# A 256-token two-part model on one core: x turned by float32 products, the gates ahead of the norms, the first doubling level by a difference

## The reference, cut to what matters

```
h = rms_norm(x, norm1_g)                        # (256, 1024)
proj = h @ w_in                                 # dn_qkv, dn_z, dn_a, dn_b, ..., fox_f, gates

def gated_deltanet(qkv, z, a_logit, b_logit, conv_w, a_log, dt_bias, out_g):
    qkv = silu(causal_depthwise_conv(qkv, conv_w))
    q = l2_norm(heads(q)) * dk ** -0.5
    k = l2_norm(heads(k))
    beta = sigmoid(b_logit)
    g = -exp(a_log) * softplus(a_logit + dt_bias)
    gc = cumsum(g)                              # inside chunks of 64 tokens
    decay = exp(gc_i - gc_j) for j <= i, else 0
    lower = where(strict, (k * beta) @ k.T * decay, 0)
    sol = triangular_solve(lower + eye(64), [v * beta, k * beta * exp(gc)])
    u, w = split(sol)
    # then a scan over the four chunks with a 128x128 state per head
```

## Time and profile before

| what | before |
|---|---|
| runs, us | 1417.14, 1419.36, 1419.49 (median 1419.36) |
| the profiled execution, us | 1417.25 |
| its span, us | 1415.4 |
| mean granted clock of TensorE | 0.972 |
| busy: TensorE, VectorE, ScalarE, GpSimd | 93%, 31%, 46%, 67% |
| DMA | 218.86 MB, mean 155 GB/s |

### The profile page before, as it was taken

The page is one execution under the profiler, slowest core; times in us unless marked ns, Lnnn a source line. Parts: engine busy times, 40 slices in busy tenths (PEclk is TensorE's granted clock), DMA queues, the critical chain, the costliest instruction groups (busy, mean ns, idle before and its releaser), DMA issues.

```text
span 1415.4 us, 19665 instructions
## 1 busy us (share of the span) xinstructions
PE 1315.2 (93%) x8226; PEld 1169.4 (83%) x8226; DVE 438.4 (31%) x769; ACT 649.5 (46%) x835; POOL 953.2 (67%) x416
## 2 busy tenths in 40 slices
PE   4989999768899999999999999999999978999997
PEld 4978977647688999889789978999878846999885
DVE  3537314524423321005554232101033445010114
ACT  5562326544544654334444444444435653443533
POOL 6745236534497888885648967886966645887984
PEclk9999999978999999999999999999999999999999
DMA  7634124322355555553435575564646423654651
GB/s 260 178 101 134 61 75 130 121 63 91 122 194 164 179 187 185 194 191 101 156 102 172 198 237 164 174 191 138 221 170 210 160 90 115 183 174 140 211 206 45
DMA packets 118092, 218.86 MB, mean 155 GB/s; under 512 B 9417, under 2 KB 18932, under 8 KB 117876
## 3 DMA queue, kind: packets, MB, share of 16 engines
q1 hardware_dynamic: 114016, 210.01, 46.3%
q10 hardware_dynamic: 3988, 7.60, 1.7%
HBM read 216.53 MB, written 1.05 MB: 154 GB/s over the span
## 4 chain that ended last, share of the span: by engine, by line
PE 81%; DVE 10%; ACT 4%; issue 2%; DMA 2%; ACTq 0%; POOL 0%; SPq 0%; DVEq 0%
PE acc L1832 12%; PE acc L1834 12%; PE acc L1835 12%; PE acc L1825 10%; PE acc L1826 10%; PE acc L1827 10%; PE pm L1840 8%; PE acc L1783 2%; PE acc L1784 2%; PE acc L1785 2%; ACT pm L544 1%; DMA raw<-in_w_in 1%; PE pm L1749 1%; ACT whi L544 1%; DVE XTlo L1032 0%
## 5 line engine op out<-in xcount | busy, mean ns | idle before, releaser
L529 POOL TENSOR_TENSOR wlo<-raw,whi 128x1024 fp32r<-128x1024 f32 (+2 forms) x412 | 953.0, 2337 | 447.7 <-ACT whi L544 446.3
L544 ACT ACTIVATE whi<-raw 128x1024 fp32r<-128x1024 f32 (+2 forms) x412 | 413.2, 1020 | 391.6 <-PE acc L1827 172.6
L1832 PE MATMUL acc<-XThi,whi 128*128 128x256 f32 x1424 | 406.5, 285 | 4.8 <-issue 2.9
L1834 PE MATMUL acc<-XTlo,whi 128*128 128x256 f32 x1424 | 404.9, 284 | 0.0
L1835 PE MATMUL acc<-XThi,wlo 128*128 128x256 f32 x1424 | 404.8, 284 | 0.0
L1832 PEld LDWEIGHTS acc<-XThi,whi 128*128 128x128 f32 x1424 | 275.4, 193 | 6.2 <-issue 3.7
L1834 PEld LDWEIGHTS acc<-XTlo,whi 128*128 128x128 f32 x1424 | 275.5, 193 | 0.2
L1835 PEld LDWEIGHTS acc<-XThi,wlo 128*128 128x128 f32 x1424 | 275.4, 193 | 0.0
L1825 PE MATMUL acc<-whi,XThi 128*128 128x512 f32 (+3 forms) x336 | 134.2, 399 | 2.9 <-POOL wlo L529 2.2
L1826 PE MATMUL acc<-wlo,XThi 128*128 128x512 f32 (+3 forms) x336 | 130.0, 387 | 0.0
L1827 PE MATMUL acc<-whi,XTlo 128*128 128x512 f32 (+3 forms) x336 | 129.5, 385 | 0.0
(11 more groups left out here) (409 smaller groups left out, 1672.6 us busy)
## 6 DMA issues: line engine op xcount, KB each, us to landing
raw<-in_w_in SPq DMA_DIRECT2D x68, 512.0 KB, 3.6
raw<-in_w_ff SPq DMA_DIRECT2D x64, 512.0 KB, 3.6
raw<-in_w_in_mix SPq DMA_DIRECT2D x44, 512.0 KB, 3.5
raw<-in_w_down SPq DMA_DIRECT2D x44, 512.0 KB, 4.3
raw<-in_w_gate SPq DMA_DIRECT2D x40, 512.0 KB, 3.5
raw<-in_w_up SPq DMA_DIRECT2D x40, 512.0 KB, 3.6
raw<-in_w_branch SPq DMA_DIRECT2D x16, 512.0 KB, 3.5
raw<-in_w_out_mix SPq DMA_DIRECT2D x16, 512.0 KB, 3.5
```

What stands on the lines that cost most here:

```text
L529: nc.gpsimd.tensor_tensor(wlo[:, u % SPLIT, 0:nk, 0:width], raw[:, u % RAW, 0:nk, 0:width], whi[:, u % SPLIT, 0:nk, 0:width].bitcast(F32), ...
L544: return nc.scalar.activation(out_, in_, func, **k)
L1832: T.matmul(o, wh[:, fs], hi[:, k, :], start=opens and f % 2 == 0, stop=False, skip_group_check=True)
L1834: T.matmul(o, wh[:, fs], lo[:, k, :], start=False, stop=False, skip_group_check=True)
```

## The change

Two things are put together. **At the start**, x comes in two halves (`x_in`, `x1_in`) and the head of the constants goes to ScalarE's queue, in front of `heads` and `o_g`. VectorE no longer scales x: it makes for each half of the tokens a 128x128 diagonal matrix, the identity (which TensorE has put into `pm`, semaphore `eye`) times the inverse roots. The turn is now a float32 product of x with this matrix. ScalarE copies the gains before it splits weights, and splits units 0 and 1, makes two groups of XThi, splits unit 2, makes the other two, and goes on. The rest of the constants comes behind unit 3. **In the delta rule**, ScalarE takes the gates' exponentials ahead of the norms, and VectorE the softplus ahead of q and k, on free columns of abc's bank of PSUM. TensorE waits for `dn_qkn` rather than `dn_rn` ahead of the sums, and their difference is taken straight from PSUM. The first level is not computed by products: with X = Y = 1, Y becomes 1 - mask, a subtraction on VectorE, and X is its transpose, 8 transposes on TensorE, which ScalarE copies into `d_x`. The fills of `d_x` and `d_y` go.

The diff, with its parts on declarations and addresses left out:

```diff
         @block.sync
         def _(sp_):
-            sp_.dma_start(X[:], a["x"].rearrange("(t p) d -> p t d", p=P)).then_inc(S["x_in"], 16)
-            sp_.dma_start(ct[:, 0:HEAD_COLS], a["consts"][:, 0:HEAD_COLS]).then_inc(S["x_in"], 16)
+            sp_.dma_start(X[:, 0, :], a["x"][0:P, :]).then_inc(S["x_in"], 16)
+            sp_.dma_start(X[:, 1, :], a["x"][P:2 * P, :]).then_inc(S["x1_in"], 16)
             for u, (w, k, nk, c0, width) in enumerate(units):
-                if u == 2:
+                if u == 4:
                     sp_.dma_start(ct[:, HEAD_COLS:], a["consts"][:, HEAD_COLS:]).then_inc(S["k_in"], 16)
                 if u >= RAW:
...
                 return fn(out_, out_, ACT.Exp, scale=-0.5)
-            act.dma_start(rowsA[0:n_a, :], a["rows_a"]).then_inc(S["c_in"], 16)
-            act.dma_start(rowsB[0:n_b, :], a["rows_b"]).then_inc(S["c_in"], 16)
+            act.dma_start(rowsA[0:n_a, :], a["rows_a"]).then_inc(S["r_in"], 16)
+            act.dma_start(rowsB[0:n_b, :], a["rows_b"]).then_inc(S["r_in"], 16)
+            act.dma_start(ct[:, 0:HEAD_COLS], a["consts"][:, 0:HEAD_COLS]).then_inc(S["id_in"], 16)
             act.dma_start(heads[:], a["heads"].partition_broadcast(P)).then_inc(S["c_in"], 16)
             act.dma_start(o_g[:], a["dn_out_norm_g"].partition_broadcast(P)).then_inc(S["c_in"], 16)
             logs()
-            act.wait_ge(S["x_in"], 32)
-            for t in range(NT):
-                last = fn(XN1[:, t, :], X[:, t, :], ACT.Square, accum_out=ss[:, t:t + 1])
-            link(last)
+            act.wait_ge(S["x_in"], 16)
+            fn(XN1[:, 0, :], X[:, 0, :], ACT.Square, accum_out=ss[:, 0:1])
+            act.wait_ge(S["x1_in"], 16)
+            link(fn(XN1[:, 1, :], X[:, 1, :], ACT.Square, accum_out=ss[:, 1:2]))
+            act.wait_ge(S["id_in"], 16)
             rstd(rs[:, 0:NT], ss[:, 0:NT], D, eps6).then_inc(S["rstd"], 1)
-            high_halves(AHEAD)
             act.wait_ge(S["cols"], 1)
             fn(colA[:], pm[:, 0, 0:n_a], ACT.Copy)
-            link(fn(colB[:], pm[:, 0, P:P + n_b], ACT.Copy))
-            fn(ea[:], headv("dn_a_log"), ACT.Exp).then_inc(S["cols"], 1)
-            turn("x1", XThi, lambda f: acol("norm1_g", f))
+            fn(colB[:], pm[:, 0, P:P + n_b], ACT.Copy).then_inc(S["cols"], 1)
+            act.wait_ge(S["cols"], 2)
+            high_halves(2)
+            turn("x1", XThi, lambda f: acol("norm1_g", f), stop=2)
+            high_halves(3)
+            turn("x1", XThi, lambda f: acol("norm1_g", f), first=2)
+            high_halves(AHEAD)
             def silu(j):
...
             fn(abc[:], accT("abc")[:, :, 0:ABC], ACT.Copy).then_inc(evac_at("abc")[0], 1)
             link(silu(2))
+            logs()
+            act.wait_ge(S["c_in"], 32)
+            fn(ea[:], headv("dn_a_log"), ACT.Exp)
+            fn(sp_y[:, :, 0:8], sp_y[:, :, 0:8], ACT.Exp, scale=-1.0)
+            fn(beta[:], abc[:, :, 4:8], ACT.Exp, scale=-1.0).then_inc(S["sp_e"], 1)
             nc.scalar.preload_act_table_set("natural_log")
             act.wait_ge(S["dn_l2"], 1)
...
             link(fn(sums, sums, ACT.Ln, bias=eps6))
             logs()
             fn(sums, sums, ACT.Exp, scale=-0.5).then_inc(S["dn_rn"], 1)
-            fn(sp_y[:, :, 0:8], sp_y[:, :, 0:8], ACT.Exp, scale=-1.0)
-            fn(beta[:], abc[:, :, 4:8], ACT.Exp, scale=-1.0).then_inc(S["sp_e"], 1)
             leave("z", zs[:], ACT.Silu)
             high_halves(begun("fq", 2) + AHEAD)
             logs()
...
             for s in range(6):
                 for hf in range(2):
                     act.wait_ge(S["dn_t1"], 2 * s + hf + 1)
-                    fn(d_t1[:, hf * W:(hf + 1) * W], pm[:, 2 * hf, :], ACT.Copy).then_inc(S["dn_t1c"], 1)
+                    fn((d_t1 if s else d_x)[:, hf * W:(hf + 1) * W], pm[:, 2 * hf, :], ACT.Copy).then_inc(S["dn_t1c"], 1)
                 high_halves(level_end(s) + AHEAD)
                 if s == 3:
                     leave("fv", fx[:, :, 2 * W:3 * W])
...
             v.wait_ge(S["rstd"], 1)
             link(variance(rv[:, 0:NT], ss[:, 0:NT], D, 1e-6))
             refine_columns(0, NT)
+            v.wait_ge(S["eye"], 1)
             for t in range(NT):
-                last = V.tensor_scalar(XN1[:, t, :], X[:, t, :], rs[:, t:t + 1], None, ALU.mult)
+                last = V.tensor_scalar(scale[:, t, :], pm[:, 3, 0:P], rs[:, t:t + 1], None, ALU.mult)
             last.then_inc(S["xn"], 1)
             v.wait_ge(S["cols"], 2)
             turn("x1", XThi, XTlo, lambda f: acol("norm1_g", f))
...
                 last = V.scalar_tensor_tensor(out=sp_y[:, :, 4 * i:4 * i + 4], in0=g, scalar=-1.0,
                                               in1=logit[:, :, 4 * i:4 * i + 4], op0=ALU.mult, op1=ALU.max)
             last.then_inc(S["sp_in"], 1)
+            v.wait_ge(S["sp_e"], 1)
+            free = acc[:, chunks["abc"][0] % 2, 0, ABC + DN_H + 4:BANK]
+            softplus = softplus_tail(logit[:, :, 0:8], sp_y[:, :, 0:8], 8, free, 0, 16)
+            V.tensor_copy(nlf[:], softplus[:, :, 4:8])
+            link(V.scalar_tensor_tensor(out=dng[:], in0=softplus[:, :, 0:4], scalar=-1.0,
+                                        in1=ea[:].unsqueeze(1).to_broadcast([P, NT, 4]), op0=ALU.mult, op1=ALU.mult))
+            plus = free[:, 0:NT * 4].rearrange("p (t h) -> p t h", t=NT)
+            link(V.tensor_scalar(plus, beta[:], 1.0, None, ALU.add))
+            V.reciprocal(beta[:], plus).then_inc(S["dn_g"], 1)
             v.wait_ge(S["dn_rn"], 1)
             V.scalar_tensor_tensor(out=qT, in0=pm[:, 0:2, :].rearrange("p a b -> p (a b)"), scalar=DH ** -0.5,
                                    in1=qT, op0=ALU.mult, op1=ALU.mult)
             V.tensor_tensor(kT, pm[:, 2:4, :].rearrange("p a b -> p (a b)"), kT, ALU.mult).then_inc(S["dn_qkn"], 1)
             v.wait_ge(S["dn_qkn"], 1)
-            v.wait_ge(S["sp_e"], 1)
-            softplus = softplus_tail(logit[:, :, 0:8], sp_y[:, :, 0:8], 8, pm[:, 3, :])
-            V.tensor_copy(nlf[:], softplus[:, :, 4:8])
-            V.scalar_tensor_tensor(out=dng[:], in0=softplus[:, :, 0:4], scalar=-1.0,
-                                   in1=ea[:].unsqueeze(1).to_broadcast([P, NT, 4]), op0=ALU.mult, op1=ALU.mult)
-            link(V.tensor_scalar(beta[:], beta[:], 1.0, None, ALU.add))
-            V.reciprocal(beta[:], beta[:]).then_inc(S["dn_g"], 1)
             v.wait_ge(S["dn_gc"], 1)
-            link(V.tensor_copy(gcs[:], pm[:, 0, 0:16].rearrange("p (k h) -> p k h", h=4)))
-            V.tensor_tensor(gcs[:, 2:4, :], gcs[:, 2:4, :], gcs[:, 0:2, :], ALU.subtract).then_inc(S["dn_gcs"], 1)
+            sums = pm[:, 0, 0:16].rearrange("p (k h) -> p k h", h=4)
+            link(V.tensor_copy(gcs[:, 0:2, :], sums[:, 0:2, :]))
+            V.tensor_tensor(gcs[:, 2:4, :], sums[:, 2:4, :], gcs[:, 0:2, :], ALU.subtract).then_inc(S["dn_gcs"], 1)
             v.wait_ge(S["dn_rows"], 1)
...
             V.tensor_tensor(d_at.rearrange("p (k s) -> p k s", s=P),
                             pm[:, 2:4, :].rearrange("p a (k s) -> p (a k) s", s=P),
                             con("tri64").unsqueeze(1).to_broadcast([P, 8, P]), ALU.mult).then_inc(S["dn_lt"], 1)
-            for x in (d_x, d_y):
-                last = V.tensor_copy(x.rearrange("p (k s) -> p k s", s=P), ident.unsqueeze(1).to_broadcast([P, 8, P]))
-            link(last)
             v.wait_ge(S["dn_kv"], 1)
             kp = ht(pm[:, 0:2, :].rearrange("p a b -> p (a b)"))
...
                                 d_lt.rearrange("p (k s) -> p k s", s=P),
                                 con(f"lvl{s}").unsqueeze(1).to_broadcast([P, 8, P]), ALU.mult).then_inc(S["dn_ml"], 1)
             level_mask(0)
-            for s in range(6):
+            v.wait_ge(S["dn_ml"], 1)
+            V.tensor_tensor(d_y.rearrange("p (k s) -> p k s", s=P), ident.unsqueeze(1).to_broadcast([P, 8, P]),
+                            d_mls[0].rearrange("p (k s) -> p k s", s=P), ALU.subtract).then_inc(S["dn_y1"], 1)
+            level_mask(1)
+            v.wait_ge(S["dn_y1"], 1)
+            level_mask(2)
+            V.tensor_tensor(qT, qT, d_egr, ALU.mult).then_inc(S["dn_y"], 1)
+            for s in range(2, 6):
                 for hf in range(2):
                     half = slice(hf * W, (hf + 1) * W)
-                    if s:
-                        v.wait_ge(S["dn_pq"], 2 * (s - 1) + hf + 1)
-                        V.tensor_tensor(d_x[:, half], d_x[:, half], pm[:, 2 * hf + 1, :], ALU.subtract)\
-                            .then_inc(S["dn_xn"], 1)
-                        V.tensor_tensor(d_y[:, half], d_y[:, half], pm[:, 2 * hf, :], ALU.subtract)\
-                            .then_inc(S["dn_xn"], 1)
+                    v.wait_ge(S["dn_pq"], 2 * (s - 2) + hf + 1)
+                    V.tensor_tensor(d_x[:, half], d_x[:, half], pm[:, 2 * hf + 1, :], ALU.subtract)\
+                        .then_inc(S["dn_xn"], 1)
```

(43 more changed lines are left out.)

8 lines of the change are left out of this document (5 added, 3 removed).

## The result

The changed kernel takes **1397.05 us** (median of 4 runs, 1395.27 to 1399.13), the kernel before 1419.4 (median of 4, 1417.14 to 1419.49). The ratio is 0.9847, with a 95% interval of 0.9829 to 0.9864: faster by 22.3 us, with 1399.5 forecast. The profiled execution took 1399.13 with a span of 1397.3; against the profiled one before (1417.25, span 1415.4) that is 18.1, with 18.7 in the sum.

A forecast was written before the change was run, and what follows sets the result against it. TensorE's work plus its standstills and slow-clock stretches bound the kernel. 6.7 + 6.3 + 5.7 = 18.7 us off the profiled 1417.25 gives 1398.6; half of 2.1 added gives 1399.5 us, range 1394.5 to 1406.5.

The forecast's parts named there:

- The start: Up to the first product matmul: it comes at 16.0 rather than 22.66, 6.7 us saved, ends 3.8 and 9.2.
- the two operations: At the start on VectorE: two 128x128 operations replace 5.66 us of scaling, a sixteenth of the elements, taken as 0.4 us.
- the turn: At the start on TensorE: 16 float32 products, 32 rows, 24 slow at 0.21 and 8 quick at 0.118, 6.0 us.
- the squares: At the start: two squares over halves of x landed by 5.9 end near 7.2, hidden behind the constants' landing at 7.6.
- The gates: At the cumulative sums: the 3.58 us wait goes, and slow-clock rows save 0.85 and 1.9; 6.3 us saved.
- The cover: At the gates: TensorE may go on at 80.8, z ends at 81.86, so 1.1 us spare; 5.3 saved if it fails.
- The first level: Delta rule: 48 rows (5.4 us) become 8 transposes (0.9), and the wait falls by 1.2 to 0.6; 5.7 us saved.
- The rule against it: First level: with GpSimd running, mask and difference, both operands in SBUF, cost 2.8 us more, leaving 2.9 saved; quiet price assumed.
- (b): Rival: the weights become the bound and it ends slower; GpSimd would need 3.6 us a unit; 3%.
- (c): Rival: another input holds the start near 19 and a late Exp takes 3 us at the gates; 1409; 4%.
- (a): Rival: terms come out small, 3.8 at the start, 5.3 at the gates, 2.9 at the first level; 1405.3; 22%.
- each saving shifts all that follows: Behind the changed places: both kernels issue the same rows in the same order, so savings carry on in full.

The follow-up runs named there:

- the start alone: The kernel before with only the start of the diff changed, and ScalarE's exponential of a_log moved from head to gates: 1411.67 us, ratio 0.9947.
- the order alone: The changed kernel, but VectorE scales x and TensorE turns it by 16 transposes as before; transfers, gains and splits stay changed: 1396.99 us, again 1396.6.
- The filled wait: The kernel before with 15 unused float32 products of constants in TensorE's wait for beta: 1415.39 us, ratio 0.998.
- GpSimd busy: The changed kernel with three extra, unused GpSimd subtractions of constants beside the first mask and difference: 1401.87 us, one run.
- the gains put back: The changed kernel, but ScalarE splits five units of weights before it copies the gains, as before: 1405.2 us, one run.
- the scaling held: The changed transfers and order with x scaled by VectorE and turned by transposes, the scaling held until ScalarE has split the first unit: 1400.05 us, one run.

## Why the prediction was right, step by step

**The start**, 6.7 forecast, 6.40 measured. The constants landed at 7.45 (7.6), the root and its refinement ended at 9.8 (9.5), the two operations took 0.61 (0.4), the turn 5.91 (6.0), with 5.66 from its start to the first product. The 0.3 of the root are a step that failed: the squares were not hidden. The second half of x ended ScalarE's wait only at 6.78 (forecast 5.9), its square with the read of the sum ended at 7.94, and the root began at 7.96, half a microsecond after the constants. The 0.4 for the two operations rested on a slip: two of 128 columns are an eighth of two of 1024, not a sixteenth. By the quiet price of the scaling an eighth is 0.18 (1.42/8), so by this estimate most of the 0.61 is fixed time. The turn and the landing were each read from a row near them and held. At 0.21 and 0.118 a row the 5.66 us from the turn to the product are about 20 slow rows and 12 quick ones, where I had put 24 and 8. In the start alone they are 6.40, so about 28 and 4, and over the six profiles with this turn they lie between 5.37 and 6.47: the number of slow rows is not fixed by the kernel, and that the split of 24 and 8 came within 0.35 is in part luck.

What failed is a step that did not enter the sum. "Instead of 5.66 us of scaling there are two operations" took the 5.66 for the price of the scaling. It was the price of scaling beside GpSimd. With the order changed both scalings are issued ahead of GpSimd's first low half and cost 1.42, and the kernel without the new product starts 1.45 earlier. I had used this very effect at the first level and had not asked it here, though the same rows show GpSimd from 10.88 on beside a scaling that begins at 10.87. The Trainium skill (SBUF — State Buffer, section Who interferes with whom) says that `tensor_scalar` can enter a mode that takes the ports shared with GpSimd, and that the one that issues first holds them for its whole instruction; the trace agrees, with 5.61 against 1.42. In the order alone it is GpSimd that is held: its low half issued at 10.73, during the second scaling, took 2.85 us, and those behind it 2.4. Who was first in the kernel before can't be told, with starts 0.01 us apart. The two copies of the identity, 5.03 for two, look like the same case; that was not tried. The sum came out right because it priced what stands there after, not what each half of the edit contributes.

**The gates**, 6.3 forecast, 6.3 measured, and in the same pieces: 3.75 of wait and its neighbours, 0.89 at the eight sums, 1.68 in fq's unit (1.9 forecast). The filled wait shows the last two to be the clock's. The cover was 0.9, near the 1.1 forecast: with the start's 6.40 taken off, the forecast has the exponentials at 65.6, the Exp on the norms at 71.9 and q and k at 74.4, and they ended at 65.6, 72.0 and 74.4. One piece was wrong, the softplus with 6.1 for 3.95, and it did no harm, because the Exp on the norms sets the end.

**The first level**, 5.7 forecast, 5.85 measured up to the second level (5.83 up to fv's unit), with the wait at 0.59 for 0.6 forecast. The rule against it is confirmed with both signs: quiet 1.21 and 1.23, busy 1.95 and 3.25 (2.61 each was forecast), and the end of the forecast that hung on it, 2.8 less, came with a wait longer by 2.8. The Trainium skill (SBUF — State Buffer, section Who interferes with whom) has it that the later of the two accesses is blocked altogether. The trace agrees: in the run with GpSimd busy the difference begins at 110.98 and ends at 114.23, past the end of GpSimd's second subtraction at 113.14 by 1.1 us, one quiet operation.

**The rivals.** (b), the weights as the bound, is refuted: no wait of TensorE in the first 140 us is for a low half of weights. (c) would have needed the start near 19; it was at 16.26, and of the kernels with the changed start only the two made for it passed 19, with the gains put back (25.40) and with the scaling held (20.51). (a) asked for terms of 3.8, 5.3 and 2.9, and none came. The 2.9 was made to happen with GpSimd busy; the other two were not tried.

**From the sum to the median.** The sum was 18.7, the profiled pair 18.1, the medians 22.3, 20.4 and 18.8 apart. I had added half of 2.1 because before's median lay above its profiled run; the changed kernel's median lay 2.1 below its own. So 18.1 against 18.7 is nearer than the mechanism deserves, and that is luck: behind the first level the changed kernel won 3.0 us more by 326.61, in stretches of lower clock that the sum had at nothing, and its profiled execution lost 2.8 again at 1067 to 1073, where its two other profiles lost 0.6 at most. The sum rests on the sentence that each saving shifts all that follows, and this holds only to about 3 us. What before's own executions give and take there is open, since only one was profiled.

## What to carry to other kernels

Before work is moved from VectorE to TensorE to shorten it, look at what GpSimd does in the same microseconds, and find the same form of instruction in a quiet place: here 5.66 us were 1.42, and the cure was the order of transfers and splits. A wait on TensorE is priced with the slower rows behind it (at the gates 3.7 of wait and 2.6 of clock, and 0.9 less of clock in another kernel with the same wait), and the rows that follow at full pace are where that price ends. When the local terms agree with their rows and the total does not, follow the distance of the same rows through several profiles of one kernel: here it kept within 0.35 us up to 1055 us and changed by 2.2 and 2.9 in one place.

## What the runs showed of the hardware

- A TENSOR_SCALAR of 128x1024 float32 from SBUF to SBUF took 0.71 us (two in 1.42) when both were issued before GpSimd began, and 2.8 (two in 5.61) beside GpSimd's subtractions: four times. A TENSOR_TENSOR of that size took 1.2 and up to 3.4.
- After idle time the rows of TensorE ran at half pace at the start (16 transposes in 3.65), and after work of TensorE at full pace (1.94 us). The clock column of the profile reads 1.00 over both stretches: at the start of an execution it is the distance of the rows that tells the clock.
- Two waits of 1.82 and 1.86 us at the same place: behind one the granted clock stayed at 1.00, behind the other it was 0.59 on average over 3 us.
- The issue of one transfer of 512 KB took ScalarE's queue 2.07 us in one execution and 0.84 in another.
